# One chip, one core: another layout for the scratch matrices that a blockwise inverse passes through memory

## The reference

```python
# per head and chunk of c tokens: k scaled, decay from the cumulated gates
a_low = jnp.where(strict, jnp.einsum('nhcid,nhcjd->nhcij', kb, k) * decay, 0.0)
tmat = lax.linalg.triangular_solve(eye + a_low, eye, left_side=True, lower=True, unit_diagonal=True)
u = jnp.einsum('nhcij,nhcjv->nhciv', tmat, v * beta[..., None])
w = jnp.einsum('nhcij,nhcjk->nhcik', tmat, kb * jnp.exp(g)[..., None])
```

## Time and profile before

| | us |
|---|---|
| Time before, median of 3 runs | 3723.0 |
| lowest and highest of the runs | 3717.28, 3728.93 |
| the profiled execution's own time | 3723.0 |
| its span | 3721.2 |
| PE busy | 3507.1 (94%) |
| DVE, ACT, POOL busy | 1484.4 (40%), 1033.5 (28%), 1344.8 (36%) |
| DMA, mean over the span | 50 GB/s |

### The profile page before, as it was taken

One profiled execution on the slowest core, in us unless ns is written; L12 is line 12 of the kernel. 1 busy time (PEld: TensorE's weight loads), 2 busy tenths in 40 slices (PEclk: granted clock), 3 DMA queues, 4 the chain that ended last, 5 costly groups with the idle time before them and its releaser, 6 DMA issues. The chain is left out here.

```text
span 3721.2 us, 45188 instructions
## 1 busy us (share of the span) xinstructions
PE 3507.1 (94%) x17736; PEld 2885.7 (78%) x17736; DVE 1484.4 (40%) x2252; ACT 1033.5 (28%) x1745; POOL 1344.8 (36%) x1164
## 2 busy tenths in 40 slices
PE   6999999999989898979999999999989999999998
PEld 5777778786778787878778878878778887777877
DVE  4232333343244444444673333333436124444343
ACT  3343433341233333332121111111122124433121
POOL 4122212123242424232434334334342445554543
PEclk9999999999999898989999999999989999999999
DMA  2000000011210101012311111111141111111122
GB/s 100 23 29 23 29 29 29 23 35 40 72 45 18 45 18 45 18 39 87 144 64 42 51 45 45 51 45 45 40 146 48 51 46 54 38 48 48 61 85 74
DMA packets 104032, 187.69 MB, mean 50 GB/s; under 512 B 32312, under 2 KB 64696, under 8 KB 101184
## 3 DMA queue, kind: packets, MB, share of 16 engines
q1 hardware_dynamic: 103872, 185.48, 15.7%
HBM read 158.33 MB, written 27.12 MB: 50 GB/s over the span
## 5 line engine op out<-in xcount | busy, mean ns | idle before, releaser
L303 PE MATMUL DP<-XH,WH 128*128 128x512 f32 x2608 | 900.7, 427 | 23.3 <-POOL WL L251 23.3
L249 POOL CAST WH<-WRAW 128x1024 fp32r<-128x1024 f32 (+2 forms) x257 | 264.0, 1027 | 1647.1 <-issue 1042.1
L303 PE MATMUL DP<-XL,WH 128*128 128x512 f32 x2608 | 815.7, 394 | 0.0
L303 PE MATMUL DP<-XH,WL 128*128 128x512 f32 x2608 | 813.4, 393 | 0.0
L303 PEld LDWEIGHTS DP<-XH,WH 128*128 128x128 f32 x2608 | 477.3, 192 | 183.1 <-issue 86.1
L251 POOL TENSOR_TENSOR WL<-WRAW,WH 128x1024 fp32r<-128x1024 f32 (+2 forms) x257 | 587.0, 2284 | 20.7
L303 PEld LDWEIGHTS DP<-XL,WH 128*128 128x128 f32 x2608 | 496.5, 190 | 108.1
L303 PEld LDWEIGHTS DP<-XH,WL 128*128 128x128 f32 x2608 | 494.9, 190 | 107.9
L836 DVE SCALAR_TENSOR_TENSOR SS<-B,RQ,SBI 128x256 f32<-128x256 f32 (+2 forms) x192 | 74.5, 430 | 383.8 <-PE B L541 383.8
L686 ACT ACTIVATE PP<-SS,NM 128x256 f32<-128x256 f32 (+2 forms) x192 | 88.5, 461 | 320.7 <-DVE NM L843 320.7
L1426 PE MATMUL DP<-YY,AA 128*128 128x64 f32 x704 | 99.9, 302 | 73.7 <-DMA YY<-yy_dram 69.5
(11 more groups left out here) (468 smaller groups left out, 5327.0 us busy)
## 6 DMA issues: line engine op xcount, KB each, us to landing
WRAW<-in_w_up SPq DMA_DIRECT2D x44, 512.0 KB, 3.5
WRAW<-in_w_attn SPq DMA_DIRECT2D x36, 512.0 KB, 3.6
WRAW<-in_w_down SPq DMA_DIRECT2D x22, 512.0 KB, 3.5
XR<-in_x SPq DMA_DIRECT2D x8, 1024.0 KB, 8.0
WRAW<-in_w_dn SPq DMA_DIRECT2D x16, 512.0 KB, 3.5
aa_dram<-AA SPq DMA_DIRECT2D x12, 512.0 KB
YY<-yy_dram SPq DMA_DIRECT2D x12, 512.0 KB, 4.0
WRAW<-in_w_lrux SPq DMA_DIRECT2D x10, 512.0 KB, 3.5
```

The lines of the kernel that those rows point to most:

```text
L249: pool.tensor_copy(WH[b.slot][:, 0:b.kt, :], WRAW[b.slot][:, 0:b.kt, :]).then_inc(w_hi, 1)
L303: mm = pe.matmul(DP[b.slot][:, half * H:half * H + H], w[b.slot][:, k, :], x[:, k, half * H:half * H + H], start=one, stop=end)
```

## The change

Both scratch tensors are stored row after row, [128, 8, 128]: what one partition of AA or YY holds is then one run of 4096 bytes in memory. The diagonal blocks of one matrix are still 64-byte pieces, but the step between matrices no longer fits the step between blocks. `diagonal` now gives the eight blocks of one matrix, so each read and write of the 64 blocks takes eight transfers of 8 partitions where it took two of 32. All waits on them count accordingly (128 where it was 32). AA is now stored as plus A: one DVE operation makes the PSC factor where two did, the corrections subtract, and POOL negates the 16x16 blocks while it copies them, with one more operation per chain (`NSTEP` 4 where it was 3).

```diff
-        aa_dram = nc.dram_tensor("aa_dram", [8, P + 1, P], F32, kind="Internal").ap()
-        yy_dram = nc.dram_tensor("yy_dram", [8, P + 1, P], F32, kind="Internal").ap()
+        aa_dram = nc.dram_tensor("aa_dram", [P, 8, P], F32, kind="Internal").ap()
+        yy_dram = nc.dram_tensor("yy_dram", [P, 8, P], F32, kind="Internal").ap()
...
-        NSTEP = 3 + 2 * 14
+        NSTEP = 4 + 2 * 14
...
-        def diagonal(dram, d):
-            return bass.AP(dram.tensor, dram.offset + 4 * P * (P + 1) * d, ap=[[16 * (P + 1), 32], [P, 16], [1, 16]])
+        def diagonal(dram, q):
+            return bass.AP(dram.tensor, dram.offset + P * q, ap=[[16 * (8 * P + 1), 8], [8 * P, 16], [1, 16]])
...
-            sp.dma_start(matrices(aa_dram), AAV[m][:, :, :, :, :].rearrange("p d e h n -> p (d e h) n")).then_inc(aa_out, 16)
+            sp.dma_start(aa_dram, AAV[m][:, :, :, :, :].rearrange("p d e h n -> p (d e h) n")).then_inc(aa_out, 16)
             sp.wait_ge(aa_out, AA0 + 16 * (c + 1))
-            sp.wait_ge(yy_out, YYO0 + 32 * c)
-            for d, t in enumerate((BL, BY)):
-                sp.dma_start(t[32 * d:32 * d + 32, :, :], diagonal(aa_dram, d)).then_inc(blk_in, 16)
+            sp.wait_ge(yy_out, YYO0 + 128 * c)
+            for q in range(8):
+                t = BW if q >= 4 else BL
+                sp.dma_start(t[8 * q:8 * q + 8, :, :], diagonal(aa_dram, q)).then_inc(blk_in, 16)
             if c:
                 sp.wait_ge(yy_in, YYI0 + 16 * c)
             sp.wait_ge(blk_ready, RDY0 + c + 1)
-            for d, t in enumerate((BY, BW)):
-                sp.dma_start(diagonal(yy_dram, d), t[32 * d:32 * d + 32, :, :]).then_inc(yy_out, 16)
-            sp.wait_ge(yy_out, YYO0 + 32 * (c + 1))
+            for q in range(8):
+                t = BW if q >= 4 else BY
+                sp.dma_start(diagonal(yy_dram, q), t[8 * q:8 * q + 8, :, :]).then_inc(yy_out, 16)
+            sp.wait_ge(yy_out, YYO0 + 128 * (c + 1))
             sp.wait_ge(v_ps, 2 * g - 2)
-            sp.dma_start(YYV[v][:, :, :, :, :].rearrange("p d e h n -> p (d e h) n"),
-                         matrices(yy_dram)).then_inc(yy_in, 16)
+            sp.dma_start(YYV[v][:, :, :, :, :].rearrange("p d e h n -> p (d e h) n"), yy_dram).then_inc(yy_in, 16)
...
-                for d in range(2):
-                    dve.scalar_tensor_tensor(out=PSC[:, 0, d], in0=beta(p)[:, d], scalar=-1.0,
-                                             in1=RK[p % 2][:, 0], op0=ALU.mult, op1=ALU.mult)
+                dve.tensor_tensor(PSC[:, 0], beta(p), rk, ALU.mult)
...
-                pool.tensor_copy(BY[lo, :, :], BL[lo, :, :].rearrange("p i j -> p j i")).then_inc(blk_step, 1)
+                pool.tensor_scalar(BY[lo, :, :], BL[lo, :, :].rearrange("p i j -> p j i"), -1.0, None, ALU.mult).then_inc(
+                    blk_step, 1)
...
-                pool.tensor_copy(BL[up, :, :], BY[up, :, :].rearrange("p i j -> p j i")).then_inc(blk_step, 1)
-                pool.wait_ge(blk_step, step(p, c, 2))
+                pool.tensor_scalar(BY[up, :, :], BW[up, :, :], -1.0, None, ALU.mult).then_inc(blk_step, 1)
+                pool.tensor_copy(BL[up, :, :], BW[up, :, :].rearrange("p i j -> p j i")).then_inc(blk_step, 1)
+                pool.wait_ge(blk_step, step(p, c, 3))
...
-                    pool.tensor_tensor(y, y, t, ALU.add).then_inc(blk_step, 1)
+                    pool.tensor_tensor(y, y, t, ALU.subtract).then_inc(blk_step, 1)
```

More of the change, by code:

```diff
@@ L1157, in chain @@
             return g // 4 * 3 + g % 4 - 1
-        def diagonal(dram, d):
-            return bass.AP(dram.tensor, dram.offset + 4 * P * (P + 1) * d, ap=[[16 * (P + 1), 32], [P, 16], [1, 16]])
-        def matrices(dram):
-            return dram[:, 0:P, :].rearrange("q r c -> r q c")
+        def diagonal(dram, q):
+            return bass.AP(dram.tensor, dram.offset + P * q, ap=[[16 * (8 * P + 1), 8], [8 * P, 16], [1, 16]])
         def blocks_sp(sp, g):
@@ L1883, in corrected @@
                         x = dve.tensor_tensor(y, y, PT_U[e][half(d), 256 + 128 * d:384 + 128 * d].rearrange(
-                            "p (h n) -> p h n", h=2), ALU.add)
+                            "p (h n) -> p h n", h=2), ALU.subtract)
                     x.then_inc(ly_ready[e], 1)
@@ L1888, in corrected @@
                 dve.tensor_tensor(y, y, PT_U[e][:, 256:512].rearrange("p (d m b) -> p d m b", d=2, b=2 << l),
-                                  ALU.add).then_inc(ly_ready[e], 1)
+                                  ALU.subtract).then_inc(ly_ready[e], 1)
             def taps(p, pos):
@@ L2060, in first_level @@
                 for d in range(2):
-                    x = pool.tensor_tensor(XX[e][:, d], twice(IDENT), XX[e][:, d], ALU.add)
+                    x = pool.tensor_tensor(XX[e][:, d], twice(IDENT), XX[e][:, d], ALU.subtract)
                 x.then_inc(x0_ready, 1)
@@ L2067, in base_blocks @@
                 lo, up = slice(0, 32), slice(32, 64)
-                pool.wait_ge(blk_in, BLK0 + 32 * (c + 1))
-                pool.tensor_copy(BY[lo, :, :], BL[lo, :, :].rearrange("p i j -> p j i")).then_inc(blk_step, 1)
+                pool.wait_ge(blk_in, BLK0 + 128 * (c + 1))
+                pool.tensor_scalar(BY[lo, :, :], BL[lo, :, :].rearrange("p i j -> p j i"), -1.0, None, ALU.mult).then_inc(
+                    blk_step, 1)
                 pool.wait_ge(blk_step, step(p, c, 1))
                 pool.wait_ge(rb_ready, min(NT * p + 2 * (g % 4) + 4, NGRP))
-                pool.tensor_copy(BL[up, :, :], BY[up, :, :].rearrange("p i j -> p j i")).then_inc(blk_step, 1)
-                pool.wait_ge(blk_step, step(p, c, 2))
+                pool.tensor_scalar(BY[up, :, :], BW[up, :, :], -1.0, None, ALU.mult).then_inc(blk_step, 1)
+                pool.tensor_copy(BL[up, :, :], BW[up, :, :].rearrange("p i j -> p j i")).then_inc(blk_step, 1)
+                pool.wait_ge(blk_step, step(p, c, 3))
                 pool.tensor_copy(BY[0:64, :, :].rearrange("p i j -> p (i j)")[:, 0:256:17], ONES[0:64, 0:16]).then_inc(
                     blk_step, 1)
-                pool.wait_ge(blk_step, step(p, c, 3))
+                pool.wait_ge(blk_step, step(p, c, 4))
                 for j in range(1, 15):
@@ L2082, in base_blocks @@
                                            [64, j, 15 - j]), ALU.mult).then_inc(blk_step, 1)
-                    pool.wait_ge(blk_step, step(p, c, 2 * j + 2))
-                    pool.tensor_tensor(y, y, t, ALU.add).then_inc(blk_step, 1)
                     pool.wait_ge(blk_step, step(p, c, 2 * j + 3))
+                    pool.tensor_tensor(y, y, t, ALU.subtract).then_inc(blk_step, 1)
+                    pool.wait_ge(blk_step, step(p, c, 2 * j + 4))
                 pool.tensor_copy(BW[up, :, :], BY[up, :, :].rearrange("p i j -> p j i")).then_inc(blk_ready, 1)
@@ L2645, in _ @@
                 sp.wait_ge(st_zero, 1)
-                sp.dma_start(matrices(yy_dram), YYV[1][:, :, :, :, :].rearrange("p d e h n -> p (d e h) n")).then_inc(yy_out, 16)
+                sp.dma_start(yy_dram, YYV[1][:, :, :, :, :].rearrange("p d e h n -> p (d e h) n")).then_inc(yy_out, 16)
                 for p in range(NPAIR):
```

## The result

The changed kernel takes 3741.6 us (median of 6 runs, 3735.5 to 3750.7) against 3724.3 us of the kernel before (median of 6, 3717.3 to 3728.9): a ratio of 1.0051, 95% interval 1.0034 to 1.0069, so 13 to 26 us slower (the two medians are 17 us apart). I had forecast 3766, with 3740 to 3796 as the range. The sign is right and the time lies at the range's low end, but the size of the change, 17 us against 43, is off by more than half. The profiled execution, which is not among the six, has a span of 3746.2 us, 25.0 more than before. All ratios in this text leave out slow executions, of which there was one: 8455 us, in neg_tensor.

What follows compares the result with a forecast made beforehand. PE is busy nearly all the span, and eight of its waits for YY are exposed. Each chain grows by 2.35 + 2.88 + 1.0 - 0.8 = 5.4 us, together 43.5 on 3723.0: 3766 us, range 3740 to 3796.

Steps and rivals of the forecast that it cites:

- What bounds the kernel: Delta rule: PE, busy nearly throughout, waits for YY's read; eight waits of about 9 us lengthen with their chains.
- Reading and writing the blocks: SP's two block stages: eight issues in place of two add 2.35 us reading and 2.88 us writing per chain.
- POOL: POOL's part of a chain: one added operation and a copy turned into TENSOR_SCALAR cost 1.0 us per chain.
- Whole matrices: Writing AA and reading YY: rows of 4096 instead of 512 bytes save 0.3 + 0.5 = 0.8 us per chain.
- Which chains count, and the cover of chain 2: Chains 1 and 3 of each pair, eight in all, count; chain 2's wait of some 3 us returns at chain 3.
- Transfers that do not overlap: Rival at the block stages: each small transfer pays its own landing, 25.5 us per chain, 3927 us; chance 0.03.
- Long rows that win: Rival at the same eight waits: whole-matrix savings exceed the cost of POOL and further issues, 3709 us; chance 0.04.
- A draw: Rival in the chains: cheap issues and helpful rows leave 1.2 us per chain, 3733 us, within 0.3%; chance 0.06.
- Slow small pieces: Rival at the block stages: memory slow at steps of 4096 bytes, landings 2 us longer each, 3798 us; chance 0.07.

Runs made afterwards that it cites:

- neg_tensor: Changed kernel with POOL's two scalings by -1 written as products with a constant tile of -1: 1.0089 of the kernel before.
- eight_old: Kernel before, old layout, with eight transfers of 8 partitions per block stage in all twelve chains: 1.0083 of the kernel before.
- four_old: Kernel before, old layout, with four transfers of 16 partitions per block stage: 1.0041 of the kernel before.
- sixteen_old: Kernel before, old layout, with sixteen transfers of 4 partitions per block stage: 1.0203 of the kernel before.
- pool_only: Changed kernel's signs, POOL and DVE operations, with the layout and two transfers per stage of the kernel before: 1.0051 of the kernel before.
- rows_only: Kernel before with the new layout but two transfers of 32 partitions per stage (inverse wrong, same amount of work): 0.9981 of the kernel before.
- eight_chain2: Kernel before, old layout, with eight transfers per stage only in the second chain of each pair: 0.9991 of the kernel before.
- eight_chains13: Kernel before, old layout, with eight transfers per stage only in the first and third chain of each pair: 1.0063 of the kernel before.
- layout_only: Changed kernel's layout and eight transfers per stage, with signs and POOL operations of the kernel before: 1.0036 of the kernel before.
- the second's 28: The changed kernel timed once more, on a second chip, against the kernel before: 1.0077, 22 to 35 us slower.
- kilobyte_rows: Kernel before with two matrices side by side (rows of 1024 bytes) and four transfers of 16 partitions per stage: 1.0024 of the kernel before.

## Why the prediction was right or wrong

*What bounds the kernel.* Right. Eight waits of PE carry the change. 8 times the growth of a chain is the growth of PE's wait, in the changed kernel (3.43 x 8 = 27.4) and in eight_old (3.17 x 8 = 25.4 against 25.4).

*Reading and writing the blocks: this step failed in its size.* I put the pitch of the issues at 0.48 us, from the run of 16 small reads the earlier trace rows, and had 2.35 + 2.88 = 5.23 us. The pitch is 0.36 us, just above my lower bound of 0.35, and the stages grew by 1.05 + 1.83 = 2.88, each of them less than my lower bound (1.37 and 1.90). Those 16 reads have 16 partitions each, and four_old has the same pitch with 16 partitions (0.49 us), though its transfers are half as large; eight_old and sixteen_old have 0.36 to 0.37 with 8 and 4. I had chosen the row by its number of bytes, and the price goes with the number of partitions. The number of pieces isn't it: the 16 reads and the transfers of sixteen_old both move 64 pieces each (of 512 and of 64 bytes), at 0.48 and 0.36 us. The pitch makes some 0.7 us of the miss in each stage. The last, smaller transfer also landed some 0.4 us sooner in both (YY's read went out 1.53 us after the eighth write in the mean, where I had 1.9). And the read stage before was 3.19 us in the mean, where I had taken 2.95 from the medians, though the chain that I had read took 3.55.

*POOL.* The operation added was right, its price too low: +1.42 us where I put 1.0. The upper bound, 1.31, came from a row of 128 partitions that is not transposed and was too low as well. pool_only shows this term alone at PE, +11.7 us.

*Whole matrices.* Right in the sum: -0.86 us in the changed kernel where I put -0.8. The split was not: writing AA gained 0.50 and reading YY 0.36, where I had 0.3 and 0.5. rows_only shows the term alone at 0.2% of the time. The Trainium skill's line rate from 512 bytes on ("DMA: Bandwidth & Descriptors", Specifications) would have it at nothing; here the measurement decides against that reading: 3.2 us against 2.6 for the same 512 KB.

*Which chains count, and the cover of chain 2.* Right, and shown by eight_chain2 and eight_chains13. The waits of chain 2 stayed smaller than I said, 0.45 us each where I had 2 to 4, since the chain grew less: its read of YY went out 1.6 us later, counted from PE's resume after chain 1, where I had about 3.5. sixteen_old shows the end of the cover, where I had put it, 5.9 us later than before (I had 5.7): SP issues chain 3's AA right behind chain 2's YY, and chain 3 pays 2 us for the transfers side by side.

*The rivals.* Transfers that do not overlap (3927 us): false, eight of them are issued and landed within 4.3 us. Long rows that win: false in sum, though true as a term. A draw (up to 11 us): excluded, on the first chip narrowly (13 us and more). Slow small pieces: false, eight_old and the changed kernel have the same stages.

So the terms are 1.05 + 1.83 + 1.42 - 0.86 = 3.4 us per chain in place of 5.4, 27 us in place of 43.5. That this sum lies inside my bounds of 2.1 to 9.0 is in part luck, since the block stages lay below theirs and POOL above its own. And that the time on the first chip lies inside the range is luck as well: it is 10 us short of what the terms give.

What remains is that distance, from 27 to 17 us. It doesn't lie in the delta rule, which the profiles show to be 25.8 and 25.9 us longer. Executions differ elsewhere too. The first product of `times_a` starts at 1017.8 us in the kernel before, but at 1004.3 in layout_only and at 1019.9 in pool_only, though the kernels do the same work up to there (eight_old and eight_chains13, which differ in the chains alone, start at 1018.2 and 1007.2):

```profile
L1423 PE MATMUL DP<-YY,AA x704: 219/275/476, 1004.3 to 1677.9; 128*128 128x64 f32 x176
```

```profile
L1426 PE MATMUL DP<-YY,AA x704: 219/275/476, 1019.9 to 1686.8; 128*128 128x64 f32 x176
```

TensorE's granted clock goes with it: it falls from its upper level (2.4 GHz, 1.00 here) to the lower one (1.2 GHz, 0.50) not only in the waits for YY. In the kernel before, for instance, it does so at 1203 us, after PE had stood still for about 1.1 us in the four before (columns as in the earlier trace rows):

```profile
1199.00:1203.00 4.00, 2.91 (x25) 2.52 (x23) 1.77 (x3) 3.39 (x4) 2.89 (x5) 1.00 0.00 0
1203.00:1207.00 4.00, 4.00 (x16) 3.35 (x15) 1.60 (x6) 0.63 (x1) 0.00 (x0) 0.58 0.00 0
```

There PE works four microseconds at little more than half its clock. Some executions have more of these places than others. An estimate of what they cost is PE's busy time times the missing share of the clock, added up over windows of 1 us. Over the first 1000 us it gives 35.7 us for the kernel before, 20.3 for layout_only and 39.1 for pool_only, which goes with the starts above. From 1000 to 1750 us it gives 34.8 us for the kernel before, 33.0 for the changed kernel and 28.0 for pool_only. With it the delta rule's length fits nearly: 25.8 us longer in the changed kernel, of which 27.4 are the wait and -1.8 the clock; 5.3 longer in pool_only's profiled execution, with 11.7 and -6.8. So executions differ by up to 16 us in a part that the change doesn't touch, more than the distance between the two chips' results. Which of the timed executions had how much of it is not on record, so what gave the first chip's runs 17 and the second's 28 stays open.

## What to carry to other kernels

Where a chain of dependent transfers ends in a wait of the busiest engine, write down its stages as start to start times and price an edit per stage: a longer run in memory (0.4 to 0.6 us for 512 KB here) is not worth six more transfers in each of two stages (2.9 us in the sum) and one more small operation. Take the price of an issue from a row with the same number of partitions, not with the same number of bytes. And look at which waits of the chain are covered by the next one before multiplying. Where the time scatters by as much as the effect, compare the length of the changed stretch in the profiles: here it gave 25.8 and 25.9 us on two chips whose timings gave 17 and 28.

## What the runs showed of the hardware

- An issue of a small transfer on SP's queue behind another takes 0.33 us for 4 and 8 partitions (sixteen_old, eight_old), 0.45 for 16 (four_old), 0.49 for 32 (before), at the same 16 pieces of 64 bytes per partition. From start to start it is 0.36 to 0.37 us with 4 and 8 and 0.49 with 16.
- 512 KB of SBUF to memory: 3.2 us to landing in runs of 512 bytes (before), 2.9 of 1024 (kilobyte_rows), 2.6 of 4096 (rows_only and the changed kernel).
- GpSimd on 32 x 256 float32: a copy that reads transposed 0.60 us, multiplication by a constant 0.84, the same with the input read transposed 1.07 (pool_only); by a broadcast tensor 0.72 and 0.85 (neg_tensor).
